# Two attentions' and many chunks' order: one half of a chunk ends first, and VectorE combines before the next maxima

## The reference, cut to what matters

```python
for l in range(DEPTH_2):
    zx = jnp.split(modulate(rms_norm_2(x, norm1_g[l]), ...) @ w_in[l], 10, axis=-1)   # context: zc
    x = x + mod_x[2] * token_mixers(zx, k1, k2, v, ...)       # four mixers, concatenated, @ w_out
    x = x + mod_x[5] * channel_mixer(modulate(rms_norm_2(x, norm2_g[l]), ...), w1, w2)
# one of the mixers, for each head and block of 128 queries over 512 + 256 keys:
p1 = softmax(q1 @ k1.T * scale); p2 = softmax(q2 @ k2.T * scale)
o  = (p1 - lam * p2) @ v
# channel mixer
square(relu(h @ w1)) @ w2          # 1024 -> 4096 -> 1024
```

## Time and profile before

| | |
|---|---|
| median of 3 runs | 2175.35 us (2169.73 to 2176.43) |
| the profiled execution, its time | 2169.36 us |
| its span, first to last instruction | 2167.6 us |
| mean granted TensorE clock | 0.986 |
| TensorE busy | 2058.6 us, 95% |
| VectorE busy | 1267.5 us, 58% |
| ScalarE busy | 793.7 us, 37% |

### The profile page before, as it was taken

One profiled execution on the slowest core, in us unless ns is written; L12 is line 12 of the kernel. 1 busy time (PEld: TensorE's weight loads), 2 busy tenths in 40 slices (PEclk: granted clock), 3 DMA queues, 4 the chain that ended last, 5 costly groups with the idle time before them and its releaser, 6 DMA issues.

```text
span 2167.6 us, 26206 instructions
## 1 busy us (share of the span) xinstructions
PE 2058.6 (95%) x11020; PEld 1747.7 (81%) x11020; DVE 1267.5 (58%) x1674; ACT 793.7 (37%) x1107; POOL 75.1 (3%) x83
## 2 busy tenths in 40 slices
PE   6999999999999989899999999999998999999998
PEld 5978877878788978788888888888787777888886
DVE  7466765866746876737546455364678655343343
ACT  4433234485343355434113122132435544232231
POOL 0000000000030000020000000001100010000001
PEclk9999999999999999999999999999999999999999
DMA  8543432524421531113223233232353222222221
GB/s 291 213 153 117 175 117 99 189 88 163 167 98 59 163 98 53 65 59 128 98 99 138 94 109 106 98 119 101 111 163 83 74 88 78 97 98 98 91 95 67
DMA packets 53077, 249.17 MB, mean 115 GB/s; under 512 B 6272, under 2 KB 10512, under 8 KB 34528
## 3 DMA queue, kind: packets, MB, share of 16 engines
q1 hardware_dynamic: 51072, 242.41, 32.3%
q10 hardware_dynamic: 1296, 2.63, 0.3%
q0 software_dynamic: 592, 2.46, 0.3%
HBM read 232.53 MB, written 12.06 MB: 113 GB/s over the span
## 4 chain that ended last, share of the span: by engine, by line
PE 83%; DVE 9%; ACT 3%; issue 3%; DMA 1%; POOL 0%; ACTq 0%; DVEq 0%; SPq 0%; POOLq 0%
PE banks L1789 69%; ACT whi_f L1938 2%; DVE wlo_f L2129 1%; DVE small L1310 1%; PE banks L619 1%; PE banks L628 1%; PE banks L1811 1%; PE banks L1812 1%; PE banks L1813 1%; PE banks L508 1%; DVE prob L1330 1%; DMA mvr<-in_mst 1%; PE banks L1843 1%; PE banks L584 1%; PE banks L583 1%
## 5 line engine op out<-in xcount | busy, mean ns | idle before, releaser
L1789 PE MATMUL banks<-hxh,whi_f 128*128 128x512 f32 x1440 | 583.8, 405 | 24.4 <-ACT hxh L1949 9.0
L1789 PE MATMUL banks<-hxh,wlo_f 128*128 128x512 f32 x1440 | 568.1, 395 | 0.0
L1789 PE MATMUL banks<-hxl,whi_f 128*128 128x512 f32 x1440 | 553.8, 395 | 0.0
L2129 DVE TENSOR_TENSOR wlo_f<-raw_f,whi_f 128x2048 fp32r<-128x2048 f32 x133 | 305.0, 2294 | 187.0 <-ACT whi_f L1938 186.9
L1938 ACT ACTIVATE whi_f<-raw_f 128x2048 fp32r<-128x2048 f32 x133 | 253.7, 1908 | 314.6 <-PE banks L1789 296.4
L1789 PEld LDWEIGHTS banks<-hxh,whi_f 128*128 128x128 f32 x1440 | 273.8, 190 | 87.4 <-issue 28.6
L1789 PEld LDWEIGHTS banks<-hxl,whi_f 128*128 128x128 f32 x1440 | 272.4, 189 | 60.2
L1789 PEld LDWEIGHTS banks<-hxh,wlo_f 128*128 128x128 f32 x1440 | 273.8, 190 | 58.3 <-issue 1.9
L1450 DVE SCALAR_TENSOR_TENSOR xT<-banks,small,xT 128x512 f32<-128x512 f32 x80 | 59.5, 749 | 264.5 <-PE banks L1789 264.5
L1789 PE MATMUL banks<-fxh,whi_f 128*128 128x512 f32 x512 | 202.3, 395 | 8.5 <-DVE cT L1450 3.9
L1789 PE MATMUL banks<-fxh,wlo_f 128*128 128x512 f32 x512 | 201.0, 393 | 0.0
(11 more groups left out here) (329 smaller groups left out, 3142.6 us busy)
## 6 DMA issues: line engine op xcount, KB each, us to landing
raw_f<-in_wst SPq DMA_DIRECT2D x133, 1024.0 KB, 4.9
mvr<-in_mst SPq DMA_DIRECT2D x120, 512.0 KB, 5.8
stack<-qk_parts SPq DMA_DIRECT2D x36, 192.0 KB, 6.7
x_kept<-xT SPq DMA_DIRECT2D x2, 2048.0 KB, 8.6
raw_f<-in_wst SPq DMA_DIRECT2D x8, 384.0 KB, 6.1
xT<-x_kept SPq DMA_DIRECT2D x2, 1536.0 KB, 8.8
qk_parts<-qk_h SPq DMA_DIRECT2D x3, 768.0 KB, 3.8
qk_parts<-qk_l SPq DMA_DIRECT2D x3, 768.0 KB, 3.6
```

The costliest lines, as they stand in the source:

```text
L1789: last = pe.matmul(o, w[:, k, c, :], r[part][:, k, :], start=(k == order[0] and i == 0), stop=(k == order[-1] and i == 2))
L2129: dve.tensor_tensor(wlo[r][:], raw[r][:], whi[n % 2 if n > N_FIRST else n][:].bitcast(F32), ALU.subtract).then_inc(w_lo, 1)
```

## The change

1. `step` takes its products as pairs (weights, activations): `HIGH` is whi·high and wlo·high, `LOW` is whi·low, `ALL` all three in the order whi·high, whi·low, wlo·high. Ordinary chunks now use `ALL`, so whi comes twice in a row.
2. `gemm` with one wait for each step (the channel mixers' second matrices and the output chunk: the wait for the low parts, which come last anyway) takes half 0 with all its products, then half 1. With two waits it does as before, but in the last step half 0 ends before half 1 begins. The first channel-mixer chunk of layer 0, written out by itself, does the same.
3. `run` on VectorE: combine(v) stands ahead of maxima(v+1), and splits and taps behind the maxima; three taps in every unit that has no split, until there are none left. The split for the seventh chunk of a layer goes from before the first maxima to behind them.

```diff
+ALL, HIGH, LOW = ((0, 0), (0, 1), (1, 0)), ((0, 0), (1, 0)), ((0, 1),)
...
-            gemm(base, 0, own, ready=[lambda k, d=d: pe.wait_ge(d, KT * l + Y_ORDER.index(k) + 1) for d in (y_hi, y_lo)],
+            gemm(base, 0, own, ready=[lambda k: pe.wait_ge(y_lo, KT * l + Y_ORDER.index(k) + 1)],
...
-                            ready = [lambda k, d=d: pe.wait_ge(d, KT * b + (KT * NFB * l + k + 1)) for d in (f_hi, f_lo)]
+                            ready = [lambda k: pe.wait_ge(f_lo, KT * b + (KT * NFB * l + k + 1))]
...
-                if j != 3:
+                if j < 3:
                     split(n + 2)
...
-            due = [None]
+            due = [base + 6]
...
                 maxima(v0)
+                weights_due()
                 for v in range(v0, v1):
                     if v + 1 < v1:
+                        upto(p.scores(v + 1))
+                    combine(v)
+                    if v + 1 < v1:
                         maxima(v + 1)
+                    splits = due[0] is not None
                     weights_due()
-                    combine(v)
                     if v0 == 0:
-                        conv(3 if v < more else 2)
+                        conv(0 if splits else 3)
                     if v in late:
                         late[v]()
...
-                if ready:
-                    for k in order:
-                        for c in range(2):
-                            ahead(k, c)
-                            if c == 0:
-                                ready[0](k)
-                            part(k, c, (0, 1))
-                        ready[1](k)
-                        for c in range(2):
-                            part(k, c, (2,))
...
+                for k in order:
+                    ahead(k, 0)
+                    if len(ready) > 1:
+                        ready[0](k)
+                        part(k, 0, HIGH)
+                        if k == order[-1]:
+                            ready[1](k)
+                            part(k, 0, LOW)
+                        ahead(k, 1)
+                        part(k, 1, HIGH)
+                        if k != order[-1]:
+                            ready[1](k)
+                            part(k, 0, LOW)
+                        part(k, 1, LOW)
+                    else:
+                        ready[0](k)
+                        part(k, 0)
+                        ahead(k, 1)
+                        part(k, 1)
```

More of the change, by code:

```diff
@@ L799, in layer @@
                     wait_high(SX, n_ff[0], k)
-                    for c in range(2):
-                        if k == 0:
+                    for c, parts in ((0, HIGH), (1, HIGH), (0, LOW), (1, LOW)) if k < KT - 1 else \
+                            ((0, HIGH), (0, LOW), (1, HIGH), (1, LOW)):
+                        if k == 0 and parts is HIGH:
                             pe.wait_ge(acc_free[c], n)
-                        step(n, 0, k, c, X, parts=(0, 1))
-                    wait_low(SX, n_ff[0], k)
-                    for c in range(2):
-                        last = step(n, 0, k, c, X, parts=(2,))
-                        if k == KT - 1:
+                        if c == 0 and parts is LOW:
+                            wait_low(SX, n_ff[0], k)
+                        last = step(n, 0, k, c, X, parts=parts)
+                        if k == KT - 1 and parts is LOW:
                             last.then_inc(acc_ready[c], 1)
@@ L1724, in ahead, with part @@
                         pe.wait_ge(acc_free[c], n if at is None else n - 3 if n < 6 else n - 1)
-                def part(k, c, parts=(0, 1, 2)):
+                def part(k, c, parts=ALL):
                     last = step(n, s, k, c, rhs, order, at and (lambda r: at(n, c)), parts)
-                    if k == order[-1] and parts[-1] == 2:
+                    if k == order[-1] and parts is not HIGH:
                         last.then_inc(acc_ready[c], 1)
-                if ready:
-                    for k in order:
-                        for c in range(2):
-                            ahead(k, c)
-                            if c == 0:
-                                ready[0](k)
-                            part(k, c, (0, 1))
-                        ready[1](k)
-                        for c in range(2):
-                            part(k, c, (2,))
-                else:
+                if not ready:
                     for c in range(2):
@@ L1745, in gemm @@
                             part(k, c)
+                    return
+                for k in order:
[17 more added lines that the diff above has]
+                        part(k, 1)
             def norm_sums(d, q, sq, slot=KT - 1):
@@ L1777, in weights, with step @@
                 pe.wait_ge(w_lo, n + 1 - N_FIRST)
-            def step(n, s, k, c, rhs, order=(0, KT - 1), at=None, parts=(0, 1, 2)):
+            def step(n, s, k, c, rhs, order=(0, KT - 1), at=None, parts=ALL):
                 wh = whi[s][:].rearrange("p (k c f) -> p k c f", k=KT, f=P)
                 wl = wlo[w_place(n)][:].rearrange("p (k c f) -> p k c f", k=KT, f=P)
-                for i in parts:
-                    w, part = ((wh, 0), (wl, 0), (wh, 1))[i]
+                for w, part in parts:
                     for r in rhs:
                         o = at(r) if at else acc[:, c, r[2]:r[2] + r[3]]
-                        last = pe.matmul(o, w[:, k, c, :], r[part][:, k, :], start=(k == order[0] and i == 0),
-                                         stop=(k == order[-1] and i == 2))
+                        last = pe.matmul(o, (wh, wl)[w][:, k, c, :], r[part][:, k, :],
+                                         start=(k == order[0] and parts is not LOW and (w, part) == (0, 0)),
+                                         stop=(k == order[-1] and parts is not HIGH and (w, part) == parts[-1]))
                 return last
@@ L1821, in _ @@
                 wait_high(SX, n_pre, k)
-                for parts in ((0, 1), (2,)):
-                    if parts[-1] == 2:
+                for parts in (HIGH, LOW):
+                    if parts is LOW:
                         wait_low(SX, n_pre, k)
@@ L1827, in _ @@
                             last = step(n, n, k, c, HX, at=lambda r: own_bank(n, c), parts=parts)
-                            if k == KT - 1 and parts[-1] == 2:
+                            if k == KT - 1 and parts is LOW:
                                 last.then_inc(acc_ready[c], 1)
```

## The result

| | before | after |
|---|---|---|
| median | 2173.77 us of 4 runs | 2146.36 us of 4 runs |
| ratio | | 0.9878, 95% interval 0.9856 to 0.9900 |
| profiled execution, its span | 2169.36, 2167.6 us | 2144.59, 2142.8 us |
| mean granted clock | 0.986 | 0.990 |

The forecast was 2150 and a gain of 24.4; the spans differ by 24.8 us.

A forecast was written before the change was run, and what follows sets the result against it. TensorE's matmuls fill 95% of the span, so only its idle time or slowed clock matters. Chunk ends 8.4 + attention 16.0 = 24.4 us off the median 2175.35 gives 2151.0, taken as 2150; range 2140 to 2163.

The forecast's parts named there:

- The chunk ends: Step-fed chunks: half 0 ends earlier, so the next chunk waits less for evictions; 8.4 us gained, bounds 0 to 9.
- Rival 3: Chunk ends give nothing because another wait is last; gain 16 us, time 2159, chance 0.08.
- The product order at nothing: Every step multiplies whi by high and low parts before wlo; costed at nothing, bounds 0 to a few ns a pair.
- The attention's net gain: Attention of both layers: 34.1 us of waits and low clock go, 16.5 come back, 1.6 charged for clock; 16.0 gained.
- the new ring: Layer 1 attention: VectorE's maxima, exponentials, combine take 5.3 us a unit; wait 0.48 becomes about 0.26 at the scores.
- The last quarters: End of each layer's attention: short convolution and last split delay maxima; scores wait 3.0 us (layer 0) and 4.7 (layer 1).
- The boundary at 761: Layer 0 chunk boundary: TensorE arrives 1.4 us earlier and waits about 3.1 us instead of 1.96, costing 1.1.
- The clock: Attention: TensorE's low clock after long waits goes, 7.2 us back; one new fall charged at 1.6.
- Rival 1: Attention: the clock falls as often as before, at other places; gain 18.8 us, time 2156, chance 0.14.
- Rival 2: Attention: the ring is 5.5 us through ScalarE's evictions between exponentials; gain 17 us, time 2158, chance 0.10.
- Rivals 3 and 4: The fourth: whi twice in a row costs time in up to 2736 pairs; 2206 us at 20 ns each, chance 0.04.
- Rival 5: Attention gains nothing and fallen clocks eat the chunk ends' gain; within 0.3%, 2172 us, chance 0.05.

The follow-up runs named there:

- x_order: The kernel before with only the product order of ordinary chunks changed (whi high, whi low, wlo high); 2172.04 us, ratio 0.9999.
- x_split_scale: x_split with ScalarE's scaling of the values moved in front of both exponentials; 2144.83 us, ratio 0.9876 to the kernel before.
- x_scale: The full change with ScalarE's scaling of the values in front of the two exponentials instead of between them; 2135.15 us, ratio 0.9839 to the kernel before.
- x_split: The full change, but combine stays behind the next maxima as before, with splits and taps behind both; 2141.48 us, ratio 0.9869 to the kernel before.
- x_attn: The kernel before with only the change's new VectorE order in the attention, chunk ends as before; 2156.61 us, ratio 0.9939.
- x_again: The full change timed once more, unchanged, on another chip; 2142.20 us, ratio 0.9861 to the kernel before.
- x_chunk: The full change with the attention's order of before, so only chunk ends and product order changed; 2157.35 us, ratio 0.9945 to the kernel before.
- x_front: The full change, but splits and taps stand behind combine and in front of the next maxima; 2200.41 us, ratio 1.0140 to the kernel before.
- x_spread: The full change with VectorE's extra work of the last quarter spread over its units; 2143.86 us, ratio 0.9871 to the kernel before.

## Why the prediction came out, point by point

**The chunk ends: right.** 8.4 us was forecast. The waits fell by 8.5: cT by 3.5, xT by 2.3, relu by 2.3, o by 0.4. The wait at 991.62 for the weight split is 1.80 as in the earlier trace rows. By its own timing the part gives 11.9 (8.0 to 16.1). Rival 3 is out. Of the two-wait chunks, o went from 1.35 to 0.89 and layer 0's av from 0.77 to 0.31, 0.46 each as forecast. The av row still rose from 2.4 to 2.6, for layer 1's av wait is sometimes 1.6 and sometimes 2.3 us, whatever the chunk ends: 2.3 in x_order, which has those of before, and 1.6 in x_split_scale, which has the new ones.

**The product order at nothing: right**, by x_order.

**The attention's net gain: about right, 13.2 (9.3 to 17.2) against 16.0; its working: half wrong.** The step that failed is the new ring, "the wait of 0.48 becomes one of about 0.26 at the scores". It is 0.43, at the turn. The ring was added up on VectorE, and I placed the scaling inside the 2.07 of the exponentials without asking who waits for it. The turn does, in the kernel: its wait for `q_on`, the count of units that are scaled, stands in `turn`. VectorE's ring was itself well sized: 1.79 from the maxima to the first exponential (1642.81 to 1644.60), 2.11 to the start of combine (1646.71) and 1.39 of combine make 5.29, where I had 5.3. But the way over the scaling and the turn is 5.41, and the longer one sets the unit. With the wait of 3.1 us over 6 behind the scaling already there before, I had a row for it and did not use it. The Trainium skill ("PSUM — Partial Sum Buffer", "PSUM bank collisions raise a hardware error") says that two engines may not touch one bank of the same partitions at the same time; the turned probabilities end and the values begin in one bank of 512 words, which would be why the kernel has this wait. No run here shows that, and the wait itself was not taken away; x_scale only fulfils it earlier.

Where the 9.4 us of waits (30.0 to 20.6) went, from the two traces:

| turns and scores, us | before | after |
|---|---|---|
| starts of the two layers | 2.5 + 4.8 | 1.8 + 3.9 |
| waits behind a split, layer 0 (1.87 and 1.88) | 3.8 | 0 |
| units of layer 1 (two of them, 1.67 and 2.77, behind a split) | 8.4 | 3.9 |
| other units of layer 0 | 1.0 | 1.0 |
| last quarters | 4.0 + 5.5 | 4.3 + 5.7 |

One of the waits behind a split, before (timeline): VectorE does the split first, then combine, and the turn waits for it.

```profile
1645.80 2.28 DVE L2129 TENSOR_TENSOR wlo_f<-raw_f,whi_f 128x2048 fp32r<-128x2048 f32 x1
...
1648.00 0.16 DVE L1324 RECIPROCAL small<-small 128x2 f32<-128x2 f32 x1
...
1649.53 0.88 PE L619 MATMUL banks<-consts,prob 128*128 128x128 f32 x6 [1.67 <-DVE prob L1330]
```

So four waits behind a split and a shorter start are the gain. The prediction named these as part of 17.3 us "of combine" and credited the order of combine and maxima; x_split shows that order worth nothing in sum. The last quarters were forecast at 7.7 and are 10.0, a little worse than before.

**The boundary at 761:** forecast 3.1, measured 2.06 (before 1.96). TensorE lost 0.89 on the way behind the scaling, so it came later. In x_scale, where that wait is gone, the boundary wait is 2.93: the reasoning held once its premise did.

**The clock:** forecast 7.2 back less 1.6, 5.6 net. It was put too high: the busy time of the same products fell by 3.7 us in layer 1 and not at all in layer 0, where the clock is 0.96 in both. The falls at 1680 and at the start of layer 1 are gone, and the one at 770.86 too, but new ones came behind the waits of 2.86 and 2.19 in the last quarters and behind the boundary (0.58 from 760 to 764), where one was charged. The two windows without the waits at their ends gave 12.5 us (4.3 + 9.4 - 1.2), some 9 of them idle time, against x_attn's 13.2 by time. Elsewhere TensorE's clock also fell less often in this pair of executions; the first block, whose waits the change hardly touches, ended 2.4 us sooner after, but only 0.2 sooner in x_again (652.83, 650.43 and 652.59), so that was scatter. It makes the close hit, 24.8 beside 24.4, partly luck: the two measurements of the full change give 26.5 (21.7 to 31.3) and 30.2 (24.5 to 35.8) by their ratios.

**The rivals.** Rival 1 (the clock falls as often, at other places) is out in layer 1 and held in layer 0. Rival 2 (the ring at 5.5) was nearly true for the loops, 5.41, yet the gain did not fall to 17: the loops were worth far less than I had put on them, and the splits more. Rivals 3 and 4 are out. Rival 5 is out.

**Still open:** why x_chunk gained some 3.5 us more than its waits, and where the last few us of difference between the spans come from; the scatter of single executions is as large.

## What to carry to other kernels

When a cycle runs over three engines, write down every wait of each member, with its releaser, before adding up a ring; a 0.3 us operation between two long ones can be the last link. Extra work on an engine that feeds the ring belongs in its idle time (here behind the maxima, while ScalarE computes exponentials); between combine and the next maxima the taps of 2.07 us cost 1.86 in every unit (x_front, 5.41 to 7.27). If two links are nearly equally late, a move that cures one shows nothing until the other is moved too: test the moves alone and together.

## What was not expected

- Two orders whose waits have different releasers (combine before or behind the maxima) wait the same 20.6 us to the tenth, though the units, the starts and the last quarters each differ by 0.5 to 1.1 us.
- At a granted clock of 1.00 throughout, the same stretch of channel mixer differed by 0.7% between two executions of the same program (474.8 and 471.4).
- The 3.2 us of waits that x_spread removed did not show in the median of its five runs, so with this scatter the waits in the trace tell more than the time.
